# Groups of two experts instead of four: picks of 112 columns in two PSUM banks

## The chip, the cores and the metric

One Trainium2 chip, one of its cores. The metric is the device time of one execution in microseconds (us), from three runs of the kernel before. All arithmetic is float32.

## The reference, cut to what matters

A trunk of two residual layers (512 tokens, width 1024) and a final norm. Every layer has a mixer and then a mixture of experts (MoE). The change touches the MoE alone:

```
g_idx  = top1(softmax(xt @ router_group))            # one of 4 groups
e_idx  = top2(e_logits inside that group)            # two of its 8 experts
for each expert e of 32:                             # xb: the tokens that chose e
    hb = silu(xb @ w_gate[e]) * (xb @ w_up[e])       # 1024 -> 512, twice
    y  = hb @ w_down[e]                              # 512 -> 1024
out[token] = sum over its two experts of gate * y
```

w_gate, w_up and w_down are 2 MB each per expert, so each of the two layers streams 32 x 6.3 MB of weights.

## The kernel before, in words

Semaphores are written out by hand; every engine has its own program, and PSUM banks are handed over by two counters per bank (`fills` and `wait_full`, `drains` and `wait_drained`; `opens` waits for the last drain before a bank is used again).

**Weights.** Nine slots in SBUF (`ring`) hold three experts' gate, up and down matrices (`EXPERT_SLOTS`). SP issues all loads in order (`moe_loads`, L467): gate and up of expert e wait until PE has finished gate and up of expert e-3, down of e until down of e-3 is finished (L514 to L519). The loads of experts 3, 4 and 5 go out in pieces, released by half-way signals (`gu_half`) and by the same ends (L495 to L513).

**Picks.** An expert's tokens are gathered on PE: for each of 8 chunks of the width and each of 4 token tiles, h (the weights, 128x128 in two halves of 64) times a selection matrix (the moving side, CAP = 56 columns for each expert), summed over the tiles. DVE makes the selection matrices (`selections`, L1845; `select`, L1663: one instruction for each tile and expert) and copies the gathered chunks from PSUM, scaled, to `xgT` (`take_pick`, L1835). Experts are treated in groups of PICK = 4, so a pick has 224 columns; a bank holds 2 chunks, so 8 chunks take banks 0 to 3. `xgT` has two buffers, by the group's parity. While PE works through group g, it picks group g+1, one bank (2 chunks) per expert: five of the eight matmul steps before the expert's `turn`, three behind it, then `out_rows` (down). The selections of group g+2 are made at the end of group g on DVE (L1934).

**The start** differs. Group 0 is picked in two parts of 112 columns: part 0 (experts 0 and 1) while the router's tiles are worked out (`pick_first`, L697), part 1 (experts 2 and 3, banks named `second`) between the turns and downs of experts 0 and 1 and behind them (`first_experts`, L886). `slot_table` (L847) makes on PE the table of which row each result goes to, and DVE turns it into addresses (`row_table`, L1865). Group 1 is picked whole in experts 2 and 3.

**The expert loop** on PE (`expert`, L897): gate_up (L822; 8 chunks x 2 matrices of 512 columns), pick, turn (4 transposes), pick, down (L837; 4 chunks x 2). DVE (`dve_expert`, L1910): product with the silu that ACT made, copy of the turned hidden rows, take_pick, its half of the output rows, selections. POOL scatters the rows (L1499).

**The end.** The last four experts (`last_experts`, L963) overlap one expert's gate_up with the other's turn; nothing is picked there, since group 7 (experts 28 to 31) was picked during experts 24 to 27.

On PE a float32 matmul shows as two instructions, and a "pair" of half-width matmuls (two column halves of the array side by side) as four; one step of a pick is such a pair.

Of the kernel before, what the change touches and what calls it, by code (L numbers as in the profile page):

```python
# [50 lines left out]
PICK = 4  # L51
# [35 lines left out]
def trunk(nc, x, cols, final_g, ab_w_in, rg_w_a, rg_w_x, bias_rev, ab_w_out, c_w_in, c_w_out, router,  # L87
          w_gate, w_up, w_down, out):
    with ExitStack() as ctx:
# [79 lines left out]
        def half_row(row, nb):  # L169
# [24 lines left out]
        me.update(carve(high, [("sel", (NT, PICK * ROW)), ("rows", (2, D)), ("hT", (FC * CAP,)), ("silu", (F,)),  # L194
                               ("hrow", (F,)), ("tab", (3, NE)), ("B", (2, NT, NE))]))
        me.update(carve(low[:, 2 * NC * PICK * CAP:], [("A", (2, NT, CAP))]))
        me.update(carve(high[:, NT * PICK * ROW + D:], [("spread", (NT, NE))]))
# [5 lines left out]
        junk2 = me["sel"].rearrange("p a b -> p (a b)")  # L203
        late_sel = me["rows"][:, 0, 0:T].rearrange("p (t s) -> p t s", t=NT)
        late_pick = low[:, 0:T]
        hT_odd = low[:, T:T + FC * CAP]
        diag = low[:, T + FC * CAP:T + FC * CAP + 3 * P].rearrange("p (k t) -> p k t", k=3)
# [80 lines left out]
        def plan_moe(l):  # L288
# [303 lines left out]
        def _(pe):  # L592
# [104 lines left out]
            def pick_first(l, t, cs=range(NC), part=0):  # L697

                pe.wait_ge(sel_ready, (l * (NE // PICK + 3)) + t + 1)
                n = 2 * CAP  # L700
                for c in cs:
                    job = ("second", l, c // 2) if part else ("pick", l, 0, c // 2)
                    if t == 0 and c % 2 == 0:
                        opens(job)
                    mm = halves(bank(job)[:, (c % 2) * n:(c % 2 + 1) * n], h_cols(t, c),
                                hx["sel"][:, t, part * n:(part + 1) * n], t == 0 and c % 2 == 0, t == NT - 1 and c % 2 == 1)
                    if t == NT - 1 and c % 2 == 1:
                        fills(mm, job)

            def pick(l, g, b, steps):  # L710

                job = ("pick", l, g, b)
# [144 lines left out]
            def first_gate_up(l):  # L857

                for e in range(2):
# [3 lines left out]
                    for b in range(4):  # L863
                        if e == 0:
                            wait_drained(pe, ("pick", l, 0, b))
# [20 lines left out]
            def first_experts(l):  # L886

                first_gate_up(l)
                for e in range(2):
                    turn(l, e)  # L890
                    pick_first(l, e, part=1)
                    out_rows(l, e)
                pick_first(l, 2, part=1)
                pick_first(l, 3, part=1)
                slot_table(l)

            def expert(l, e):  # L897

                g, q = e // PICK, e % PICK
                three = EXPERT_SLOTS[e % 3]  # L900
                for s, k in e_in[l * NE + e][0:2]:
                    pe.wait_ge(ring_in[s], 16 * k)
                opens(("gu", l, e))
                if e == 2:
                    for b in range(4):
                        wait_drained(pe, ("second", l, b))
                    gate_up(l, three, g % 2, q, range(0, 4)).then_inc(gu_half, 1)
                    fills(gate_up(l, three, g % 2, q, range(4, 8)), ("gu", l, e))
                else:
                    if q == 0:  # L910
                        for b in range(4):
                            wait_drained(pe, ("pick", l, g, b))
                    fills(gate_up(l, three, g % 2, q), ("gu", l, e))
                if e == 3:
                    pick(l, 1, 2, range(0, 8))
                    turn(l, e)
                    pick(l, 1, 3, range(0, 8))
                    out_rows(l, e)
                    return
                b = 0 if e == 2 else q  # L920
                pick(l, g + 1, b, range(0, 5))
                turn(l, e)
                pick(l, g + 1, b, range(5, 8))
                out_rows(l, e)
                if e == 2:
                    pick(l, 1, 1, range(0, 8))
# [36 lines left out]
            def last_experts(l):  # L963

                a, b, c, d = range(NS, NE)
                for n in range(4):
# [9 lines left out]
                more_blocks(l)  # L976
                last_gate_up(l, c, range(0, 4))
# [74 lines left out]
            def moe(l):  # L1052
                pick_first(l, 3)
                first_experts(l)
                for e in range(2, NS):
                    expert(l, e)
# [531 lines left out]
        def _(dve):  # L1588
# [237 lines left out]
            def take_first(l, b, part):  # L1826

                job = ("second", l, b) if part else ("pick", l, 0, b)
# [435 lines left out]
```

## Time and profile before

| | |
|---|---|
| median of 3 runs | 1595.73 us (1593.35 to 1598.78) |
| the profiled execution | 1596.03 us, its span 1593.6 us |
| granted TensorE clock, mean | 0.994 |
| PE busy | 1537.7 us, 96% |
| DVE, ACT, POOL busy | 35%, 22%, 13% |
| DMA | 471.97 MB, mean 296 GB/s |

The span is what the profile covers; the 2.4 us between it and the execution's own time lie around it. The chain that ended last reaches back only through the final norm's last 3 us, so it does not tell what sets the time; the stages have to be read one by one. Layer 0's experts run from about 272 to 728 us, layer 1's from about 1115 to 1571 us. The two stretches are built alike.

### The profile page before, as it was taken

The page shows a single profiled execution, that of the slowest core. Times are in us where ns is not written, and L with a number is a line of the kernel's source. Part 1 is how long each engine was busy: PE and PEld are TensorE (multiplying, and loading weights), DVE is VectorE, ACT ScalarE, POOL GpSimd, SP SyncE. Part 2 cuts the span into 40 slices and gives each one's busy share as a digit, 9 for nine tenths or more (in the row PEclk, how much of TensorE's full clock was granted, in tenths as well). Part 3 has the DMA queues.
Part 4 walks back from the last instruction along what each step waited for, and adds up shares of the span by engine and source line. Part 5 has one row for each costly group of instructions (what it writes and reads, how often), then busy time and mean ns, then how long its engine had stood idle before and what let it go on. Part 6 is the DMA issues. An engine that isn't in the chain of part 4 may idle for free. (4 is left out here: it accounts for less than half of the span.)

```text
span 1593.6 us, 23381 instructions
## 1 busy us (share of the span) xinstructions
PE 1537.7 (96%) x9800; PEld 745.2 (47%) x9800; DVE 552.7 (35%) x1285; ACT 346.0 (22%) x577; POOL 210.4 (13%) x256
## 2 busy tenths in 40 slices
PE   7999999999999999988999999999999999999987
PEld 4444545544444444423566666645544444444422
DVE  4222636332222122125244444446332222122115
ACT  3131621100000000003444555432010000000003
POOL 5000000000000000000244444420000000000000
PEclk9999999999999999999999999999999999999999
DMA  8611056999999999997421112124999999999996
GB/s 314 247 62 53 27 229 273 409 367 426 428 427 427 427 426 427 427 422 316 185 81 54 54 62 95 58 95 183 375 360 427 427 426 427 427 427 428 426 422 275
DMA packets 59388, 471.97 MB, mean 296 GB/s; under 512 B 12929, under 2 KB 12937, under 8 KB 31376
## 3 DMA queue, kind: packets, MB, share of 16 engines
q1 hardware_dynamic: 54336, 462.51, 70.5%
q0 software_dynamic: 4800, 7.87, 1.3%
q8 instruction: 80, 1.31, 0.3%
q14 instruction: 28, 0.23, 0.0%
q10 hardware_dynamic: 144, 0.05, 0.0%
HBM read 452.03 MB, written 24.27 MB: 299 GB/s over the span
## 5 line engine op out<-in xcount | busy, mean ns | idle before, releaser
L827 PE MATMUL ps<-sb_ring,sb_work 128*56 128x512 f32 x2048 | 456.4, 598 | 21.1 <-issue 18.0
L827 PEld LDWEIGHTS ps<-sb_ring,sb_work 128*56 128x56 f32 x2048 | 147.6, 131 | 315.2 <-issue 314.8
L842 PE MATMUL ps<-sb_ring,sb_work 128*56 128x512 f32 x1024 | 230.9, 593 | 0.6 <-DMA sb_ring<-in_w_down_dram 0.6
L662 PE MATMUL ps<-sb_work,sb_h 128*64 128x224 f32 (+1 forms) x2304 | 218.1, 334 | 0.0
L1499 POOL DMA_INDIRECT expert_rows<-sb_work,sb_ri x60 | 54.9, 915 | 1118.2 <-DVE sb_work L1900 1105.5
L1891 DVE TENSOR_TENSOR sb_work<-sb_work,ps 56x512 f32<-56x512 f32 x64 | 69.3, 1083 | 336.3 <-ACT sb_work L1314 336.2
L662 PEld LDWEIGHTS ps<-sb_work,sb_h 128*64 128x64 f32 x2304 | 152.4, 137 | 63.9 <-issue 31.8
L1081 PE MATMUL ps<-sb_work,sb_ring 128*128 128x512 f32 x384 | 172.3, 603 | 2.0 <-ACT sb_work L1211 2.0
L1314 ACT ACTIVATE sb_work<-ps 56x512 f32<-56x512 f32 x64 | 37.7, 589 | 457.7 <-PE ps L827 457.7
L842 PEld LDWEIGHTS ps<-sb_ring,sb_work 128*56 128x56 f32 x1024 | 69.7, 130 | 119.4 <-issue 112.8
L1329 ACT ACTIVATE sb_work<-ps 56x512 f32<-56x512 f32 x60 | 35.5, 591 | 373.6 <-PE ps L842 373.6
L1081 PEld LDWEIGHTS ps<-sb_work,sb_ring 128*128 128x128 f32 x384 | 71.7, 191 | 86.9 <-issue 86.0
L735 PE MATMUL ps<-sb_work,sb_ring 128*128 128x512 f32 x256 | 110.3, 592 | 1.6 <-DVE sb_work L1611 1.6
L1900 DVE COPY sb_work<-ps 56x512 f32<-56x512 f32 x60 | 41.6, 693 | 191.2 <-ACT sb_work L1329 191.2
L735 PEld LDWEIGHTS ps<-sb_work,sb_ring 128*128 128x128 f32 x256 | 48.6, 190 | 62.6 <-issue 62.6
L2163 DVE COPY_PREDICATED sb_ring<-sb_tables,ps 128x512 f32<-128x512 uint32 x48 | 35.5, 740 | 93.0 <-PE ps L1099 92.2
L662 PE MATMUL ps<-sb_ring,sb_work 128*64 128x128 f32 x1120 | 64.3, 273 | 0.0
L662 PEld LDWEIGHTS ps<-sb_ring,sb_work 128*64 128x64 f32 x1120 | 60.9, 137 | 1.9 <-issue 1.9
L1548 POOL TENSOR_TENSOR sb_ring<-sb_ring 128x256 f32<-128x256 f32 x56 | 48.3, 863 | 88.9 <-ACT sb_ring L1384 50.4
L627 PE MATMUL ps<-sb_ring,sb_work 128*128 128x512 f32 x128 | 59.5, 599 | 0.0
L1665 DVE TENSOR_SCALAR sb_work<-sb_iota,sb_slot_key,sb_rstd 128x56 f32<-128x56 f32 x256 | 58.2, 302 | 0.3
L627 PE MATMUL ps<-sb_ring 128*128 128x512 f32 x128 | 57.8, 598 | 0.0
(241 smaller groups left out, 1198.6 us busy)
## 6 DMA issues: line engine op xcount, KB each, us to landing
sb_ring<-in_w_down_dram SPq DMA_DIRECT2D x62, 2048.0 KB, 23.5
sb_ring<-in_w_gate_dram SPq DMA_DIRECT2D x54, 2048.0 KB, 21.0
sb_ring<-in_w_up_dram SPq DMA_DIRECT2D x54, 2048.0 KB, 25.7
sb_ring<-in_w_gate_dram SPq DMA_DIRECT2D x18, 1024.0 KB, 10.7
sb_ring<-in_w_up_dram SPq DMA_DIRECT2D x18, 1024.0 KB, 28.8
sb_ring<-in_c_w_in_dram SPq DMA_DIRECT2D x8, 2048.0 KB, 8.8
sb_ring<-in_ab_w_in_dram SPq DMA_DIRECT2D x5, 2048.0 KB, 11.4
expert_rows<-sb_work SPq DMA_DIRECT2D x2, 4096.0 KB, 20.6
```

What stands on the lines that cost most here:

```text
L627: mm = nc.tensor.matmul(bank(job)[:], y[:, c, t * P:(t + 1) * P], wblock(s, NC)[:, c, :], start=(c == 0), stop=(c == NC - 1))
L662: mm = nc.tensor.matmul(dst[64 * z:64 * z + 64], a[:, 64 * z:64 * z + 64], b, start=start, stop=stop)
L735: mm = nc.tensor.matmul(dst[:], a, b, start=(c == 0), stop=(c == NC - 1))
L827: mm = nc.tensor.matmul(dst[64 * z:64 * z + CAP, :], me["xgT"][:, j, c, q * CAP:(q + 1) * CAP], wblock(slots[z], NC)[:, c, :], start=(c == ...
L842: mm = nc.tensor.matmul(dst[64 * z:64 * z + CAP, :], src[:, c * CAP:(c + 1) * CAP], wblock(slots[2], FC)[:, c, z * 512:(z + 1) * 512], sta ...
L1081: mm = nc.tensor.matmul(dst[:], w[:, c, k, :], xT[:, c, :], start=(c == 0), stop=(c == NC - 1))
L1314: A(me["silu"][64:64 + CAP, :], bank(("gu", l, e))[0:CAP, :], ACT.Silu).then_inc(silu_ready, 1)
L1499: return g.indirect_dma_start(out=y_d[l], out_offset=bass.IndirectOffsetOnAxis(ap=idx, axis=0), in_=me["rows"][0:CAP, j, :], in_offset=Non ...
L1548: g.tensor_tensor(qk[:, :, 0:m], kk[:, :, 0:m], e[:, :, 0:m], ALU.mult)
L1665: return v.tensor_scalar(dst, iota[:, 0:CAP], slot_key[:, t, e:e + 1], rstd[:, 2 * l + 1, t:t + 1], ALU.is_equal, ALU.mult)
L1891: return v.tensor_tensor(me["hrow"][0:CAP, :].rearrange("p (c q) -> p c q", c=FC), chunked(me["silu"][64:64 + CAP, :], FC), chunked(ps[moe ...
L1900: drains(v.tensor_copy(half_row(me["rows"][0:CAP, e % 2, :], 1), chunked(bank(("dn", l, e))[64:64 + CAP, :])), ("dn", l, e))
```

## The change

PICK becomes 2: a group is two experts, a pick has 112 columns, and a bank holds 4 chunks (CB), so 8 chunks take two banks (PB). One of these banks, 16 steps, is picked per expert. The cut of group 0 into two parts goes away: group 0 is now what part 0 was, and group 1 (experts 2 and 3) is an ordinary group picked in experts 0 and 1, all 16 steps between turn and down. From expert 2 on, 10 steps stand ahead of the turn and 6 behind it. `slot_table` moves behind expert 2's gate_up. The group of experts 30 and 31 is picked in `last_experts`, one bank behind the gate_up of each of experts 28 and 29, and DVE takes it there. The `sel` buffer is half as large, and a few buffers of the low region lie elsewhere.

```diff
-PICK = 4
+PICK = 2
+PB = 2
+CB = NC // PB
@@ plan_moe
             for g in range(NE // PICK):
-                for b in range(4):
+                for b in range(PB):
                     bk.add(("pick", l, g, b), moe_bank(l, b))
-                if g == 0:
-                    for b in range(4):
-                        bk.add(("second", l, b), moe_bank(l, b))
@@ pick
-                    c, t = 2 * b + i // NT, i % NT
-                    mm = halves(bank(job)[:, (c % 2) * PICK * CAP:(c % 2 + 1) * PICK * CAP], h_cols(t, c),
-                                me["sel"][:, t, 0:PICK * CAP], i == 0, i == 2 * NT - 1)
-                if steps[-1] == 2 * NT - 1:
+                    c, t = i // NT, i % NT
+                    mm = halves(bank(job)[:, c * n:(c + 1) * n], h_cols(t, CB * b + c), me["sel"][:, t, 0:n],
+                                i == 0, i == CB * NT - 1)
+                if steps[-1] == CB * NT - 1:
                     fills(mm, job)
@@ expert (PE), now for every e below NS; first_experts is gone
+            def expert(l, e):
+
+                g, q = e // PICK, e % PICK
+                if e >= 2:
+                    three = EXPERT_SLOTS[e % 3]
+                    for s, k in e_in[l * NE + e][0:2]:
+                        pe.wait_ge(ring_in[s], 16 * k)
+                    opens(("gu", l, e))
+                    if q == 0:
+                        for b in range(PB):
+                            wait_drained(pe, ("pick", l, g, b))
+                    mm = gate_up(l, three, g % 2, q, range(0, 4))
+                    if e == 2:
+                        mm.then_inc(gu_half, 1)
+                    fills(gate_up(l, three, g % 2, q, range(4, 8)), ("gu", l, e))
+                    if e == 2:
+                        slot_table(l)
+                    pick(l, g + 1, q, range(0, 10))
                     turn(l, e)
+                    pick(l, g + 1, q, range(10, 16))
                 else:
                     turn(l, e)
+                    pick(l, g + 1, q, range(0, 16))
                 out_rows(l, e)
@@ last_experts (PE)
                 last_gate_up(l, a, range(0, 8))
+                pick(l, NK // PICK, 0, range(0, 16))
                 last_gate_up(l, b, range(0, 4))
                 last_turn(l, a)
                 last_gate_up(l, b, range(4, 8))
+                pick(l, NK // PICK, 1, range(0, 16))
                 last_down(l, a, range(0, 3))
...
                 more_blocks(l)
+                for n in range(PB):
+                    wait_drained(pe, ("pick", l, NK // PICK, n))
                 last_gate_up(l, c, range(0, 4))
@@ take_pick (DVE)
-                g8 = fg[:, l, 2 * b:2 * b + 2].unsqueeze(2).broadcast_to([P, 2, PICK * CAP])
+                g8 = fg[:, l, CB * b:CB * b + CB].unsqueeze(2).broadcast_to([P, CB, PICK * CAP])
@@ dve_expert (DVE)
                 if e == 0:
                     hidden(l, 1)
+                take_pick(l, g + 1, q)
                 if e == 1:
                     slot_lists(l)
-                    for b in range(4):
-                        take_first(l, b, 1)
                     row_table(l)
-                if 2 <= e < NE - PICK:
-                    for b in {2: (0,), 3: (1, 2, 3)}.get(e, (q,)):
-                        take_pick(l, g + 1, b)
@@ moe (DVE)
-                for b in range(4):
-                    take_first(l, b, 0)
+                for b in range(PB):
+                    take_pick(l, 0, b)
```

## Rows read from the trace of the kernel before

**Rows 1.** The page's slices, 40 equal parts of the span: what the DMA engines moved.
```profile
GB/s 314 247 62 53 27 229 273 409 367 426 428 427 427 427 426 427 427 422 316 185 81 54 54 62 95 58 95 183 375 360 427 427 426 427 427 427 428 426 422 275
```

**Rows 2.** Timeline of PE, one expert of layer 0: start, us, line, count [idle before].
```profile
363.28 7.04 PE L827 MATMUL ps<-sb_ring,sb_work 128*56 128x512 f32 x32
370.15 2.06 PE L662 MATMUL ps<-sb_work,sb_h 128*64 128x224 f32 x20
372.22 0.42 PE L833 MATMUL ps<-sb_ident,sb_work 56*128 56x56 f32 x4
372.57 1.35 PE L662 MATMUL ps<-sb_work,sb_h 128*64 128x224 f32 x12
373.76 3.60 PE L842 MATMUL ps<-sb_ring,sb_work 128*56 128x512 f32 x16
377.19 7.04 PE L827 MATMUL ps<-sb_ring,sb_work 128*56 128x512 f32 x32
```

**Rows 3.** The same timeline: gate_up of experts 25 and 28.
```profile
628.46 7.08 PE L827 MATMUL ps<-sb_ring,sb_work 128*56 128x512 f32 x32 [0.75 <-issue]
...
673.64 7.08 PE L827 MATMUL ps<-sb_ring,sb_work 128*56 128x512 f32 x32 [1.21 <-DMA sb_ring<-in_w_up_dram]
```

**Rows 4.** Windows: stretch, us, engines' busy us (instructions), PEclk, DMA share, GB/s.
```profile
320.00:325.00 5.00, 5.00 (x26) 1.50 (x22) 0.00 (x0) 0.00 (x0) 0.00 (x0) 1.00 0.74 291
325.00:330.00 5.00, 5.00 (x52) 3.44 (x50) 1.99 (x3) 0.59 (x1) 0.00 (x0) 1.00 0.69 229
```

**Rows 5.** Timeline of SP's DMA issues, layer 0, experts 5 (down), 6 and 7.
```profile
315.76 0.33 SPq L458 DMA_DIRECT2D sb_ring<-in_w_down_dram  x1
325.65 0.33 SPq L458 DMA_DIRECT2D sb_ring<-in_w_gate_dram  x1
...
335.68 0.33 SPq L458 DMA_DIRECT2D sb_ring<-in_w_down_dram  x1
342.54 0.33 SPq L458 DMA_DIRECT2D sb_ring<-in_w_gate_dram  x1
```

**Rows 6.** Timeline of PE at the start of layer 0's experts.
```profile
264.12 1.13 PE L662 MATMUL ps<-sb_rt,sb_work 128*64 128x36 f32 x32
265.05 1.76 PE L662 MATMUL ps<-sb_work,sb_h 128*64 128x112 f32 x32
...
269.38 3.29 PE L662 MATMUL ps<-sb_work,sb_h 128*64 128x112 f32 x64
272.50 13.90 PE L827 MATMUL ps<-sb_ring,sb_work 128*56 128x512 f32 x64
...
300.44 0.41 PE L851 MATMUL ps<-sb_work,sb_ones 128*128 128x32 f32 x2
...
301.52 0.64 PE L827 MATMUL ps<-sb_ring,sb_work 128*56 128x512 f32 x1
```

**Rows 7.** Timeline of DVE, layer 0: first take, slot table, output rows, selections of one group.
```profile
271.64 1.47 DVE L1832 TENSOR_TENSOR sb_work<-ps,sb_fg 128x224 f32<-128x224 f32 x4 [0.16 <-PE ps L662]
...
301.82 0.19 DVE L1870 TENSOR_REDUCE sb_top<-ps 128x1 f32<-128x32 f32 x1 [0.89 <-PE ps L853]
...
303.04 0.69 DVE L1900 COPY sb_work<-ps 56x512 f32<-56x512 f32 x1
...
312.33 0.62 DVE L1842 TENSOR_TENSOR sb_work<-ps,sb_fg 128x448 f32<-128x448 f32 x1 [0.90 <-PE ps L662]
...
336.98 3.61 DVE L1665 TENSOR_SCALAR sb_work<-sb_iota,sb_slot_key,sb_rstd 128x56 f32<-128x56 f32 x16
```

**Rows 8.** Timeline of PE in the last experts, layer 0 (683 to 703), layer 1 (1547).
```profile
683.88 5.34 PE L827 MATMUL ps<-sb_ring,sb_work 128*56 128x512 f32 x16 [3.16 <-issue]
...
689.53 3.65 PE L827 MATMUL ps<-sb_ring,sb_work 128*56 128x512 f32 x16
...
702.91 10.66 PE L827 MATMUL ps<-sb_ring,sb_work 128*56 128x512 f32 x48 [2.34 <-issue]
...
1547.25 12.21 PE L827 MATMUL ps<-sb_ring,sb_work 128*56 128x512 f32 x48 [3.17 <-issue]
```

More of the change, by code:

```diff
@@ L193, in trunk @@
         me = carve(low, [("xgT", (2, NC, PICK * CAP))])
-        me.update(carve(high, [("sel", (NT, PICK * ROW)), ("rows", (2, D)), ("hT", (FC * CAP,)), ("silu", (F,)),
+        me.update(carve(high, [("junk", (D,)), ("rows", (2, D)), ("hT", (FC * CAP,)), ("silu", (F,)),
                                ("hrow", (F,)), ("tab", (3, NE)), ("B", (2, NT, NE))]))
+        me.update(carve(high, [("sel", (NT, PICK * ROW))]))
         me.update(carve(low[:, 2 * NC * PICK * CAP:], [("A", (2, NT, CAP))]))
-        me.update(carve(high[:, NT * PICK * ROW + D:], [("spread", (NT, NE))]))
+        me.update(carve(high[:, 2 * D:], [("spread", (NT, NE))]))
         fin_g = tables[:, 0:D]
@@ L695, in positions, with pick_first @@
                 fills(mm, ("pos", l, t))
-            def pick_first(l, t, cs=range(NC), part=0):
+            def pick_first(l, t, cs=range(NC)):
                 pe.wait_ge(sel_ready, (l * (NE // PICK + 3)) + t + 1)
-                n = 2 * CAP
+                n = PICK * CAP
                 for c in cs:
-                    job = ("second", l, c // 2) if part else ("pick", l, 0, c // 2)
-                    if t == 0 and c % 2 == 0:
+                    job = ("pick", l, 0, c // CB)
+                    if t == 0 and c % CB == 0:
                         opens(job)
-                    mm = halves(bank(job)[:, (c % 2) * n:(c % 2 + 1) * n], h_cols(t, c),
-                                hx["sel"][:, t, part * n:(part + 1) * n], t == 0 and c % 2 == 0, t == NT - 1 and c % 2 == 1)
-                    if t == NT - 1 and c % 2 == 1:
+                    mm = halves(bank(job)[:, (c % CB) * n:(c % CB + 1) * n], h_cols(t, c), hx["sel"][:, t, :],
+                                t == 0 and c % CB == 0, t == NT - 1 and c % CB == CB - 1)
+                    if t == NT - 1 and c % CB == CB - 1:
                         fills(mm, job)
             def pick(l, g, b, steps):
-                job = ("pick", l, g, b)
+                job, n = ("pick", l, g, b), PICK * CAP
                 if steps[0] == 0:
@@ L863, in first_gate_up @@
                     for b in range(4):
-                        if e == 0:
-                            wait_drained(pe, ("pick", l, 0, b))
+                        if e == 0 and b % 2 == 0:
+                            wait_drained(pe, ("pick", l, 0, b // 2))
                         mm = gate_up(l, EXPERT_SLOTS[e], 0, e, (2 * b, 2 * b + 1), 6 if e else 7)
@@ L884, in out_rows @@
                 fills(down(l, EXPERT_SLOTS[e % 3]), ("dn", l, e))
[L886 to L895, printed above, removed]
             def expert(l, e):
                 g, q = e // PICK, e % PICK
[L900 to L904, printed above, removed]
-                    for b in range(4):
-                        wait_drained(pe, ("second", l, b))
-                    gate_up(l, three, g % 2, q, range(0, 4)).then_inc(gu_half, 1)
-                    fills(gate_up(l, three, g % 2, q, range(4, 8)), ("gu", l, e))
-                else:
-                    if q == 0:
-                        for b in range(4):
[L912 to L915, printed above, removed]
-                    turn(l, e)
[L917 to L923, printed above, removed]
@@ L924, in expert @@
                 out_rows(l, e)
-                if e == 2:
-                    pick(l, 1, 1, range(0, 8))
             def last_gate_up(l, e, cs):
@@ L976, in last_experts @@
                 more_blocks(l)
+                for n in range(PB):
+                    wait_drained(pe, ("pick", l, NK // PICK, n))
                 last_gate_up(l, c, range(0, 4))
@@ L1053, in moe @@
                 pick_first(l, 3)
-                first_experts(l)
-                for e in range(2, NS):
+                first_gate_up(l)
+                for e in range(NS):
                     expert(l, e)
@@ L1823, in _ @@
             mixer_end(0)
-            def take_first(l, b, part):
-                job = ("second", l, b) if part else ("pick", l, 0, b)
-                wait_full(dve, job)
-                n = 2 * CAP
-                g8 = fg[:, l, 2 * b:2 * b + 2].unsqueeze(2).broadcast_to([P, 2, n])
-                drains(v.tensor_tensor(me["xgT"][:, 0, 2 * b:2 * b + 2, part * n:(part + 1) * n],
-                                       bank(job)[:, 0:2 * n].rearrange("p (c s) -> p c s", c=2), g8, ALU.mult), job)
             def take_pick(l, g, b):
@@ L1958, in last_experts @@
                 last_turned(l, a)
+                take_pick(l, NK // PICK, 0)
                 last_hidden(l, b)
                 last_turned(l, b)
+                take_pick(l, NK // PICK, 1)
                 out_rows(l, a)
```

17 lines of the change are left out of this document (8 added, 9 removed).

## The prediction

> **What bounds the kernel now.** The page says PE 96% busy, which invites the wrong answer. I read the 40 slices next: in both stretches of experts the DMA engines moved 422 to 428 GB/s in slice after slice, nine in the first [rows 1]. So PE and the weight stream are both near their limit, and only the timeline tells which one ends last. Early on, PE goes from one expert's gate_up to the next in 377.19 - 363.28 = 13.91 us with no idle time [rows 2]. Later, from expert 25 to 28, it takes (673.64 - 628.46) / 3 = 15.06 us, and PE is idle 0.75 to 1.21 us ahead of the gate_up, which ends with the load of the up matrix [rows 3]. An expert's weights are three loads of 2048 KB, 6.29 MB, and 6.29 MB at 427 GB/s [rows 1] are 14.7 us. So PE asks for weights faster than they come from the start, lives on what the ring holds, and has used it up some 20 experts later. From then on the **weight stream sets the end** of each MoE, and PE's idle time in it (ten us or so per layer) costs nothing. What counts is how early the stream becomes unbroken. It is not unbroken at first: between 320 and 330 us it moved 291 and 229 GB/s [rows 4].
>
> **The picks themselves.** Before, an expert's share of picks is 32 instructions of 224 columns: 372.22 - 370.15 plus 373.76 - 372.57 = 3.26 us, 102 ns each [rows 2]. After, it is 64 of 112 columns. The trace has those: 64 took 272.50 - 269.38 = 3.12 us, 49 ns each [rows 6]. So 3.1 to 3.2 against 3.26: nothing lost, 0.1 us of PE won per expert, hidden behind the stream. Columns in all are the same. Twice as many weight loads is no bound, since 32 instructions of the same form with 36 columns went by in 265.05 - 264.12 = 0.93 us, 29 ns each, loads included [rows 6].
>
> The Trainium skill (TensorE: Matmul & The Clock Gate, Back-to-back issue gap) says that in a stream of weight load and matmul pairs 128 columns sustain about 81 ns per matmul, because the load counts too. By that an estimate for 64 of them is 5.2 us. The row disagrees, at 49 ns for 112; it is a rival below.
>
> DVE takes 448 columns per expert before and after (0.62 us), on the same place behind the turn [rows 7]; selections are half as many, twice as often. Both lie under gate_up (6.87 us, 363.28 to 370.15) and down (3.43 us) [rows 2]. Cost nothing; if that cover were gone, 0.62 per two experts. POOL's scatters and SP's order of loads are unchanged.
>
> **Start of a MoE.** (a) Gate_up of expert 0 waited for a first take of 224 columns that needed two chunks; now it needs four chunks and a take of 0.62 us. Four chunks are full 0.8 us into the last tile's pick, which is 1.56 us long; with the 0.3 us that the first take lagged in the trace and 0.62 it is 0.2 us late: bounds 0 and 0.4, I take **+0.2**. Halved selections in the router's stage save DVE time ahead of a wait for PE: nothing.
> (b) Expert 0 and 1: the picks between turn and down are 64 instructions each instead of 32, and the 64 behind down of expert 1 go. Same sum. slot_table (301.52 - 300.44 = 1.1 us) leaves too [rows 6], so gate_up of expert 2 starts at about 300.4 instead of 301.5 and ends at 307.3.
> (c) Then slot_table, to 308.4, and then **a new wait**. The pick of group 2 needs its selections. On DVE these stand behind row_table, which waits for slot_table, and behind expert 1's output rows. From slot_table's start to DVE's first instruction it is 301.82 - 300.44 = 1.38 us, row_table 303.04 - 301.82 = 1.22, output rows 0.66, eight selections half of 3.61 = 1.8: 5.1 us, of which PE works 1.1. PE waits **4.0 us**, till 312.4. Queued behind it on PE: turn, pick and down of expert 2; SP then issues expert 5's down late. DVE needs expert 2's hidden product (1.1 us) next, ready before the turn.
> (d) After idle times of 3.16 and 3.17 us PE ran slow for a while: 5.34 against 3.65 us for 16 instructions, 12.21 against 10.66 for 48; after 2.34 us it did not [rows 8]. So the wait costs a further 0 to 1.6 us; as 4.0 is longer than 3.16, likelier the latter.
> (e) Removed from experts 2 and 3: half their picks, 6.5 us (they picked four experts' worth, now two). Net by the start of expert 4: PE is 1.1 + 6.5 - 1.1 - 4.0 - (0 to 1.6) = 2.5 to 0.9 us ahead, less (a).
>
> **What this does to the stream.** Loads go out when PE ends something [rows 5]. After (without (a)): down of 2 ends 312.4 + 3.6 (pick, turn, pick) + 3.4 = 319.4, with the slow clock 321.0; SP 0.2 later. Then +6.87 for gate_up of 3, +7.0 for its rest, +6.87 for gate_up of 4. The issues:
>
> expert 5 down: 315.76 before, 319.6 to 321.2 after.
> expert 6 gate, up: 325.65, then 326.5 to 328.1.
> expert 6 down: 335.68, then 333.5 to 335.1.
> expert 7 gate, up: 342.54, then 340.4 to 342.0.
>
> Now the queue. 291 GB/s over 5 us are 3.4 us of flow, so it ran dry at 323.4; 229 GB/s are 2.7 us, so flow resumed at 327.3, 1.7 us after the issue [rows 4, 5]. A 2 MB load flows 4.9 us. Before: 6 gate and up 327.3 to 337.1, down to 342.0, then idle to 342.54 + 1.7 = 344.2, unbroken from there. After: without expert 5's down the queue is dry at 318.5; that load flows from 321.3 (322.9) to 326.2 (327.8); 6 gate and up from 328.2 (329.8) to 338.0 (339.6); down follows at once to 342.9 (344.5), and 7 gate and up follows at once. So the unbroken stream starts 1.3 us earlier, or 0.3 later. With (a): -1.1 to +0.5. I take **-0.4 us per layer**, near the middle because (d) leans late while the small dips of a short queue, which I don't count, lean early. Layer 1 is built alike.
>
> **End of a MoE.** The pick of experts 30 and 31 moves here, 2 x 3.15 us of PE. The first falls in the idle 3.16 us ahead of expert 29's gate_up, the second is made up in the idle 2.34 (3.17) us ahead of expert 30's [rows 8]. In layer 0 that is 6.3 us of work against 5.5 of idle time; but with the first gap filled the slow clock behind it (1.7 us) goes too, so gate_up of 30 waits for its weights as before: 0. If that cover were gone, 6.3 us per layer. The loads for expert 31's down, released by down of 28 some 1.4 us later, still find a full queue.
>
> **Sum:** 2 x (-0.4) = -0.8 us on the profiled 1596.03, so 1595.2; the median of the runs is 0.3 lower, 1595.73, which gives 1594.9. I say **1595.0**. Bounds of the costs: -2.2 to +1.0. The runs spread by 2 to 3 us on either side, and about 0.3% (4.8 us) is what a measurement can tell from no change.
>
> **Rivals.**
> 1. *Faster* (0.12): the wait in (c) is cheaper, or moved work keeps the queue from running dry at all. The idle flow to be won is 3.9 us plus 2.2 us per layer by the sum above; all of it is 12 us: 1584. Half is 1590. For: PE is ahead by expert 4. Against: expert 5's down is issued late by exactly the wait.
> 2. *Slower* (0.10): the moved picks aren't covered at the end. Place: PE in the last four experts. Price: up to 6.3 us per layer, 12.6 in all, 1608; if only the second pick is exposed, 3.15 each, 1602. It decides when PE reaches expert 29 with less than about 1 us of idle ahead, that is if the ring isn't used up by then. Against: PE waits for weights from expert 25 at the latest [rows 3].
> 3. *Slower, weight loads bound the picks* (0.02). The point is a period of 15 us: 6.87 + 0.36 + 3.43 = 10.66 without picks, so 64 instructions must take 4.3 us, 68 ns each. If one of 112 columns took what one of 224 takes, 102 ns, the period would be 17.2, and the 23 experts from 5 to 27 cost 23 x (17.2 - 13.9) = 76 us, less the ten that PE idles now: 66 per layer, 1728. By the 81 ns of the Trainium skill (the same page and section) it is an estimate of 15.8 us per expert, some 35 per layer, about 1666. The trace speaks against both, with 49 ns.
> 4. *The change doesn't do what it says*: were the wait in (c) absent because DVE had its selections ready, -2.9 per layer from (c) to (e) would be capped by the queue, 1591; it is part of 1.
>
> **Numbers.** My forecast 0.76. The likeliest cases give 1592.5 to 1597.5 with the runs' spread; reaching to half of rival 1 and of rival 2's smaller price, 1590.5 to 1599.5. Chances: faster 0.13, same 0.75, slower 0.12.
>
> **What the profile would show.** Right: 64 instructions of 112 columns in 3.1 to 3.2 us per expert and a period of about 13.85 us, later 15.0 to 15.1; PE idle about 4 us per layer behind slot_table, ended by DVE's selections; the flow broken near 319 us and again near 327, whole from about 328; no gap ahead of expert 29's gate_up. Wrong: a longer period at the end, gate_up of 30 later in relation to 29's, or an unbroken stream from 300 us on.

## The result and the profile after

| | before | after |
|---|---|---|
| median | 1595.69 us (1593.35 to 1598.78, 7 runs) | 1600.95 us (1598.27 to 1603.03, 7 runs) |
| ratio to before | 1 | 1.003, 95% interval 1.0018 to 1.0042 |
| the profiled execution, its span | 1596.03, 1593.6 us | 1600.95, 1598.6 us |
| granted TensorE clock, mean | 0.994 | 0.994 |

The forecast was 1595.0 with 1590.5 to 1599.5; the change costs 5.3 us, 0.3%, and lies 1.4 us above the range. The times of the parts that I looked at most were right. PE's timeline behind expert 1 of layer 0, which answers to [rows 2, 6], and two rows of layer 1:

```profile
300.45 7.04 PE L828 MATMUL ps<-sb_ring,sb_work 128*56 128x512 f32 x32
307.42 0.41 PE L852 MATMUL ps<-sb_work,sb_ones 128*128 128x32 f32 x2
...
312.56 4.00 PE L663 MATMUL ps<-sb_work,sb_h 128*64 128x112 f32 x40 [3.79 <-DVE sb_work L1653]
316.49 0.67 PE L834 MATMUL ps<-sb_ident,sb_work 56*128 56x56 f32 x4
317.09 1.97 PE L663 MATMUL ps<-sb_work,sb_h 128*64 128x112 f32 x24
...
322.33 7.03 PE L828 MATMUL ps<-sb_ring,sb_work 128*56 128x512 f32 x32
329.20 2.08 PE L663 MATMUL ps<-sb_work,sb_h 128*64 128x112 f32 x40
...
331.61 1.37 PE L663 MATMUL ps<-sb_work,sb_h 128*64 128x112 f32 x24
...
336.24 1.03 PE L828 MATMUL ps<-sb_ring,sb_work 128*56 128x512 f32 x4
...
1158.38 3.62 PE L663 MATMUL ps<-sb_work,sb_h 128*64 128x112 f32 x40 [3.75 <-DVE sb_work L1653]
...
1552.65 12.21 PE L828 MATMUL ps<-sb_ring,sb_work 128*56 128x512 f32 x48 [2.90 <-issue]
```

Gate_up of expert 2 starts at 300.45 (300.4 was forecast), the wait for DVE's selections is 3.79 us (4.0), it ends at 312.56 (312.4). Behind it the same 68 instructions that take 2.08 + 0.42 + 1.37 us an expert later take 4.00 + 0.67 + 1.97: the slow clock costs 2.8 us (the granted clock of 315 to 320 us is 0.66, below: part of this stretch ran at 1.2 instead of 2.4 GHz). Gate_up of expert 3 follows at 322.33; before it was 318.57.

What SP issued and what the DMA engines then moved (columns as in [rows 4]); they answer to [rows 4, 5]:

```profile
322.54 0.33 SPq L459 DMA_DIRECT2D sb_ring<-in_w_down_dram  x1
329.41 0.33 SPq L459 DMA_DIRECT2D sb_ring<-in_w_gate_dram  x1
...
336.45 0.33 SPq L459 DMA_DIRECT2D sb_ring<-in_w_down_dram  x1
343.32 0.33 SPq L459 DMA_DIRECT2D sb_ring<-in_w_gate_dram  x1
```

```profile
315.00:320.00 5.00, 5.00 (x52) 3.92 (x50) 1.02 (x2) 0.00 (x0) 0.00 (x0) 0.66 0.73 294
320.00:325.00 5.00, 5.00 (x26) 1.56 (x24) 0.69 (x1) 2.40 (x4) 0.00 (x0) 1.00 0.31 69
325.00:330.00 5.00, 5.00 (x40) 2.05 (x38) 0.00 (x0) 1.56 (x2) 0.91 (x1) 1.00 0.89 375
330.00:335.00 5.00, 5.00 (x68) 3.32 (x66) 2.84 (x8) 0.01 (x1) 0.00 (x0) 1.00 0.96 342
```

There are two gaps, as the prediction had it, but each issue is 1.3 us later than the late end of its range (321.2, 328.1, 335.1, 342.0), and so the second gap reaches beyond 330 us, where the prediction had the flow whole from about 328.

Two moments of each MoE tell where the time went: the start of gate_up of expert 28, which waits for its up matrix, and the first instruction of the late add (L1005 before, L993 after), both counted from the start of gate_up of expert 0. Ahead of them stands what the DMA engines moved in the 60 us from the 30th to the 90th behind that start. As windows (the last number is GB/s; times 60 us it is MB), first before, then after, layer 0 and 1:

```profile
302.50:362.50 60.00, 59.98 (x396) 28.72 (x394) 17.92 (x48) 6.91 (x10) 4.75 (x5) 1.00 0.95 382
1144.60:1204.60 60.00, 59.99 (x396) 28.77 (x394) 17.92 (x49) 6.92 (x10) 4.62 (x5) 1.00 0.94 376
```

```profile
302.61:362.61 60.00, 56.21 (x468) 29.19 (x466) 17.46 (x50) 6.91 (x10) 4.76 (x5) 0.94 0.91 370
1148.47:1208.47 60.00, 56.23 (x474) 28.60 (x472) 17.47 (x50) 6.92 (x10) 4.63 (x5) 0.97 0.93 380
```

The same for the kernels of this study that bear on it (layer 0 / layer 1; "in all" is the median against the before of the same session):

| kernel | MB moved, 30 to 90 us | gate_up of 28 | late add | in all, us |
|---|---|---|---|---|
| before | 22.92 / 22.56 | 401.14 / 403.23 | 456.24 / 458.31 | |
| after | 22.20 / 22.80 | 404.35 / 403.20 | 460.09 / 459.83 | +5.3 |
| after again | 22.62 / 22.56 | 403.34 / 404.00 | 459.17 / 460.90 | +5.0 |
| table first | 24.78 / 24.96 | 399.08 / 398.29 | 453.67 / 456.31 | -5.5 |
| selections early | 24.36 / 24.48 | 398.73 / 399.12 | 454.58 / 454.91 | -1.6 |
| before, with a wait | 20.28 / 20.52 | 407.20 / 407.39 | 462.43 / 462.53 | +11.4 |
| before, picks split | 22.38 / 22.80 | 403.11 / 402.77 | 459.04 / 457.14 | +1.6 |
| after, no end picks | 22.02 / 22.62 | 404.30 / 403.31 | 459.69 / 457.91 | +1.2 |
| table first, no end picks | 24.60 / 24.72 | 398.79 / 399.47 | 453.43 / 454.56 | -4.9 |
| before, no overflow branch | 22.74 / 22.98 | 401.15 / 402.96 | 456.80 / 460.27 | -1.5 |
| after, no overflow branch | 22.44 / 22.68 | 403.20 / 403.49 | 458.34 / 457.93 | +3.4 |
| before, more waits on TensorE | 22.98 / 23.16 | 402.74 / 402.19 | 458.49 / 455.97 | +0.1 |

For the change the late add comes on average 2.7 us later (459.96 against 457.28), and again 2.8 in the repeat: two layers make 5.4 to 5.5 us, which is the difference of the medians. So nothing that costs time lies outside the two MoEs. These are readings of one execution each: before's own two layers, built alike, differ by 2.1 us at gate_up of 28 and at the late add. So a difference of less than about 1 us in one row of the table proves little; the means of the repeat agree with the first profile's to 0.1 us.

### The profile page after: what moved, and what is told of

It reads as the page before. It is cut to its first block, busy times and chain, and to the rows that moved or that the text cites. A ratio compares the mean times of both kernels' runs of the same rounds, so it can differ in the third digit from the quotient of the medians.

```text
span 1598.6 us, 26973 instructions
## 1 busy us (share of the span) xinstructions
PE 1541.1 (96%) x11592; PEld 794.2 (50%) x11592; DVE 554.0 (35%) x1277; ACT 346.0 (22%) x577; POOL 211.0 (13%) x256
## 3 DMA queue, kind: packets, MB, share of 16 engines
q8 instruction: 94, 1.54, 0.4%
## 4 chain that ended last, share of the span: by engine, by line
PE 49%; DMA 3%; DVE 2%; issue 1%; ACT 1%; POOLq 0%; SPq 0%; DVEq 0%; ACTq 0%
PE ps L828 13%; PE ps L663 11%; PE ps L1069 11%; PE ps L843 6%; PE ps L628 4%; DMA sb_ring<-in_w_up_dram 2%; PE ps L1087 2%; DMA sb_ring<-expert_rows 1%; PE ps L834 1%; PE ps L1128 0%; PE ps L993 0%; DVE sb_h L2027 0%; PE ps L1004 0%; ACT sb_work L1199 0%; PE ps L1096 0%
## 5 line engine op out<-in xcount | busy, mean ns | idle before, releaser
L663 PE MATMUL ps<-sb_work,sb_h 128*64 128x112 f32 x4096 | 224.3, 263 | 7.5 <-DVE sb_work L1653 7.5
L663 PEld LDWEIGHTS ps<-sb_work,sb_h 128*64 128x64 f32 x4096 | 206.5, 139 | 42.2 <-issue 30.8
L1821 DVE TENSOR_TENSOR sb_work<-ps,sb_fg 128x448 f32<-128x448 f32 x64 | 40.0, 625 | 58.4 <-PE ps L663 58.1
## 6 DMA issues: line engine op xcount, KB each, us to landing
sb_ring<-in_w_gate_dram SPq DMA_DIRECT2D x18, 1024.0 KB, 10.8
```

Source lines behind the costliest of these rows:

```text
L663: mm = nc.tensor.matmul(dst[64 * z:64 * z + 64], a[:, 64 * z:64 * z + 64], b, start=start, stop=stop)
L1821: drains(v.tensor_tensor(me["xgT"][:, g % 2, CB * b:CB * b + CB, :], bank(job)[:, 0:CB * PICK * CAP].rearrange("p (c s) -> p c s", c=CB), ...
```

## The experiments

**Where the wait stands.** slot_table goes back ahead of expert 2's gate_up, as it stood before; all else is the changed kernel.

```diff
                 g, q = e // PICK, e % PICK
+                if e == 2:
+                    slot_table(l)
                 if e >= 2:
                     three = EXPERT_SLOTS[e % 3]
...
                     fills(gate_up(l, three, g % 2, q, range(4, 8)), ("gu", l, e))
-                    if e == 2:
-                        slot_table(l)
                     pick(l, g + 1, q, range(0, 10))
```

> The changed kernel with slot_table put back ahead of gate_up of expert 2, so that DVE's row_table, output rows and selections run under that gate_up. T1 (the new wait of PE behind slot_table, 3.8 us per layer and 1.5 to 2.8 us of slow clock behind it, sends the loads of experts 5 to 7 late and so sets the whole loss): the wait is gone, down of expert 2 ends near 315 us instead of 322, gate_up of 3 near 322.5; the weight stream is unbroken some 3 us per layer earlier than in the kernel before. Time about 1590, against 1595.7 before and 1601 for the changed kernel. T2 (the picks moved into the last four experts set the loss): the wait goes, but the time stays at 1599 to 1601. T3 (picks in 112 columns slow the stream or PE by themselves): 1598 to 1601.

1590.14 us (1588.61 to 1591.33), ratio 0.9965 (0.9952 to 0.9978). PE's timeline:

```profile
300.45 0.41 PE L852 MATMUL ps<-sb_work,sb_ones 128*128 128x32 f32 x2
...
308.45 2.16 PE L663 MATMUL ps<-sb_work,sb_h 128*64 128x112 f32 x40
...
315.60 7.04 PE L828 MATMUL ps<-sb_ring,sb_work 128*56 128x512 f32 x32
```

No wait, no slow clock, gate_up of expert 3 at 315.60 instead of 322.33, and 24.9 MB in the opening 60 us instead of 22.5. 2.4 MB at 427 GB/s are 5.6 us per layer; the late add comes 5.0 earlier, twice that is 10, the medians differ by 10.8. So moving that one table decides the sign of the change: with it in its old place the groups of two are 0.35% faster than before, and this is the fastest kernel of the study, together with its variant without end picks.

**The wait shortened.** In the changed kernel the selections of group 2 are made on DVE ahead of `slot_lists`, in the time in which DVE was idle.

```diff
@@ dve_expert
                 if e == 1:
+                    selections(l, 2)
                     slot_lists(l)
...
-                if q == PICK - 1 and g + 2 < NE // PICK:
+                if q == PICK - 1 and e > 1 and g + 2 < NE // PICK:
```

> The changed kernel with the eight selections of group 2 made ahead of slot_lists instead of behind row_table and the output rows; slot_table stays behind gate_up of expert 2. T1: the pick follows slot_table at once; the next wait is at the turn of expert 2, for DVE's hidden product, which stands behind row_table, the output rows: about 1 us, too short for the slow clock. Time 1591 to 1592, nearly as with the table put first (1590.1). Against T1: 1597 or more.

1593.58 us (1590.17 to 1597.2, 12 runs), ratio 0.999 (0.998 to 0.9999). What is left is a wait at the turn, for the hidden product, which stands behind the table on DVE:

```profile
312.00 0.43 PE L834 MATMUL ps<-sb_ident,sb_work 56*128 56x56 f32 x4 [1.22 <-DVE sb_work L1870]
```

The turn's four instructions at 0.43 us are at the full clock: 1.22 us of idle time don't bring the slow one. Its row in the table promises more than 1.6 us; but the profiled execution took 1590.25 us and was among the fastest of the twelve, so the row flatters it. By the ratios the leftover wait costs 0.25% against the kernel with the table first (0.999 and 0.9965), 4.0 us.

**The wait alone.** The kernel before, with a wait of about the same length at the same place: 40 more selections on DVE, for which PE waits behind expert 2's gate_up.

```diff
@@ expert (PE), behind gate_up
+                if e == 2:
+                    pe.wait_ge(again, l + 1)
@@ dve_expert, e == 1
+                    for n in range(40):
+                        q2 = n // NT % PICK
+                        ins = select(l, n % NT, PICK + q2, me["sel"][:, n % NT, q2 * CAP:(q2 + 1) * CAP])
...
+                    ins.then_inc(again, 1)
```

> The kernel before with a wait put in behind gate_up of expert 2: DVE repeats 40 selections (same values) after expert 1's output rows, and PE waits for them ahead of the pick, about 4 us and the slow clock behind it. T1: a late start of the loads passes into the end one for one, as nothing else is removed: 6 us per layer, 1605 to 1608. If the ring's reserve absorbed such a wait (against T1): 1596 to 1598.

1607.01 us (1604.05 to 1611.85), ratio 1.0077 (1.006 to 1.0094): 11.4 us for two waits.

```profile
313.97 3.68 PE L663 MATMUL ps<-sb_work,sb_h 128*64 128x224 f32 x20 [4.16 <-DVE sb_work L1668]
```

3.68 instead of 2.06 us [rows 2]: 1.6 us of slow clock. 4.16 + 1.6 = 5.8 per layer, 11.6 in all; 11.4 are measured, with 9.6 to 15 by the interval. The opening moved 2.3 MB less, 5.5 us, and the late add is 5.2 us later. **Time that PE loses here passes almost whole into the end**, although PE idles for ten us per layer later on.

**The picks' width alone.** The kernel before, each pick of 224 columns as two of 112.

```diff
@@ pick
-                    mm = halves(bank(job)[:, (c % 2) * PICK * CAP:(c % 2 + 1) * PICK * CAP], h_cols(t, c),
-                                me["sel"][:, t, 0:PICK * CAP], i == 0, i == 2 * NT - 1)
+                    n, at0 = 2 * CAP, (c % 2) * PICK * CAP
+                    for k in range(2):
+                        mm = halves(bank(job)[:, at0 + k * n:at0 + (k + 1) * n], h_cols(t, c),
+                                    me["sel"][:, t, k * n:(k + 1) * n], i == 0 and k == 0, i == 2 * NT - 1 and k == 1)
```

> The kernel before with every pick of 224 columns issued as two of 112, everything else as it was (experts 4 to 31; as many instructions and weight loads as in the changed kernel, the same place and banks). T1 and T2: no difference that can be measured, 1595 to 1596.5; PE's distance between experts stays at 13.9 us. T3: this alone makes 1598 to 1601.

1597.24 us (1594.48 to 1599.46), ratio 1.0009 (1.0 to 1.0017). PE's timeline of one expert; the next gate_up is 13.94 us behind the first:

```profile
363.13 7.04 PE L829 MATMUL ps<-sb_ring,sb_work 128*56 128x512 f32 x32
370.00 2.09 PE L662 MATMUL ps<-sb_work,sb_h 128*64 128x112 f32 x40
372.08 0.42 PE L835 MATMUL ps<-sb_ident,sb_work 56*128 56x56 f32 x4
372.44 1.37 PE L662 MATMUL ps<-sb_work,sb_h 128*64 128x112 f32 x24
```

On PE the halves cost nothing, as the prediction said. Yet all together they may: up to 0.17%. The table shows a trace of it. Take the MB of the opening at 427 GB/s as the time by which gate_up of 28 should move against before (means of the two layers). The two kernels with 224 columns come out at -0.4 (before with a wait) and +0.2 us (before without the branch). The eight profiles with 112 columns come out later than that by 0.4 to 1.5 us, 0.9 on average.

**Is it the code?** The picks are twice as many instructions, and these have to be fetched: the page's instruction queue q8 shows 94 packets and 1.54 MB after, 80 and 1.31 before, and 95 with the picks split. Three kernels add satisfied waits to the kernel before, on one engine each.

```diff
@@ GpSimd, behind each scatter
+                    for _ in range(192):
+                        pool.wait_ge(made, 1)
```

> The kernel before with 192 further instructions on GpSimd behind the scatter of each expert, each a wait that is satisfied already. They move no data and compute nothing; their code has to be fetched. What it is for: the kernel with halved picks and nothing else (3592 instructions more on TensorE's side) was 1.0009 times before, with an interval of 1.0 to 1.0017. Theory A: the fetch of code takes its share of the weight stream. Then three times as many added instructions cost three times as much, 3 to 6 us (1599 to 1602), the profile's instruction queue shows about 0.7 MB more than its 1.31 MB, and gate_up of expert 28 in layer 1 starts 1.5 us or more later in relation to expert 0 than before's 403.2. Theory B: the fetch costs nothing that can be seen and the 1.5 us of the halved picks are something else: 1595 to 1597, ratio 1.000, the relative start of gate_up(28) unchanged.

1616.46 us (1613.57 to 1618.71), ratio 1.0126 (1.011 to 1.0141): 20.7 us, far more than theory A had. The loads that SP issued between 500 and 560 us, before and here (where they are issued, and issue to landing):

```profile
L458 SPq DMA_DIRECT2D sb_ring<-in_w_down_dram x5: 327/328/328, 502.6 to 558.2; - x5
...
DMA to landing us min/median/max: 23.4/27.1/31.5
```

```profile
L458 SPq DMA_DIRECT2D sb_ring<-in_w_down_dram x5: 328/328/328, 502.7 to 558.4; - x5
...
DMA to landing us min/median/max: 27.5/32.5/38.1
```

Issued at the same times, with 427 and 428 GB/s moved in that stretch, they land 5.4 us later; by expert 28 gate_up is 9.4 us behind in layer 0 and 6.7 in layer 1. So the bytes flow, but not those that the next load needs to be complete.

```diff
@@ ScalarE, act_expert
+                if e >= 2:
+                    for _ in range(192):
+                        act.wait_ge(slots_hot, l + 1)
```

> The kernel before with 192 satisfied waits per expert on ScalarE, which is busy 4 us in 50 there; the same number on GpSimd cost 20.7 us for 45 more packets of code of 8 KB, 0.37 MB, which at the rate of the stream (427 GB/s) would be 0.9 us. Theory A1: a packet of code goes through one of the 16 DMA engines, and every weight load ends when the last of the engines has ended its share, so a byte of code costs as much as 16 bytes spread over all. By that 0.37 MB cost 14 us on one engine, 20.7 with what waits behind each; the same on ScalarE costs 10 to 22 us, if its code comes through an engine that is as loaded as the others. Theory A2: the cost hangs on the one engine behind GpSimd's queue, which has the scatter to carry too; ScalarE's code costs 0 to 3 us. Theory C: the waits hold up GpSimd itself and its scatters, and it is not the code: 0 here, and the number of code packets rises all the same.

1612.67 us (1611.68 to 1614.37), ratio 1.0105 (1.009 to 1.012). The number is what theory A1 gave, but the number alone is a trap, for PE waits for something else:

```profile
506.96 2.06 PE L662 MATMUL ps<-sb_work,sb_h 128*64 128x224 f32 x20
509.83 0.42 PE L833 MATMUL ps<-sb_ident,sb_work 56*128 56x56 f32 x4 [0.82 <-DVE sb_work L1894]
...
690.61 10.47 PE L827 MATMUL ps<-sb_ring,sb_work 128*56 128x512 f32 x48
```

ScalarE's silu comes late behind its own added waits, DVE's product after it, and PE's period is 14.6 to 14.7 us. Gate_up of 28 (with the first half of 29's) follows at 690.61 without a wait, so PE's start does not tell what the loads did; their landings in the trace do. Counted from the start of gate_up of expert 0 as in the table, the up matrix of expert 28 has landed (layer 0 / layer 1) at:

| kernel | up of 28 landed, us | code packets more than before |
|---|---|---|
| before | 400.90 / 402.99 | |
| waits on GpSimd | 410.28 / 409.65 | 45 on q14, 0.37 MB |
| waits on ScalarE | 411.19 / 409.66 | 39 on q14, 0.32 MB |
| waits on TensorE (next run) | 402.50 / 401.95 | 6 on q8, 0.10 MB |

With the waits on ScalarE the loads lag as they do with the waits on GpSimd, again at an unchanged rate (426 GB/s from 500 to 560 us, 427 from 600 to 660). So it is not GpSimd's place in front of its scatters (C), and A2's 0 to 3 us doesn't hold for the loads; the page counts the code of both engines on the same queue, q14. A1 is left standing for q14. As a price for every byte of code it does not: by its 14 us for 0.37 MB, an estimate, the 15 packets of 16 KB more on q8 would cost the split picks 9 us, and these measured 1.6. And of the 16.6 us here the loads' lag and PE's own period can't be told apart, since PE is 3.4 and 4.9 us later than the load that it would otherwise wait for.

```diff
@@ expert (PE), at its end
+                if e >= 5:
+                    for _ in range(64):
+                        pe.wait_ge(sel_ready, 1)
```

> The kernel before with 64 satisfied waits per expert on TensorE, experts 5 to 27 of both layers, behind the work of each expert, where TensorE has 1.1 us of idle time per expert to lose before it falls behind the weights. It asks what TensorE's own code costs, which is what the halved picks add. Theory A (the fetch of TensorE's code slows the stream): the more packets on its queue cost what the 15 packets of the halved picks did (1.6 us, interval 0 to 2.7) in proportion to their number. Theory B: TensorE's code costs nothing, and the time stays at 1595 to 1597. Where the waits themselves take more than 1.1 us per expert the period shows it, and the kernel is slower by that; then only the start of the loads tells.

1596.13 us (1594.49 to 1598.31, 12 runs), ratio 1.0004 (0.9996 to 1.0013), with 6 code packets more on q8. No cost that the measurement can tell; the interval doesn't exclude 0.6 us (6/15 of 1.6) either. By the measure used for the split picks (opening against gate_up of 28) its loads are 1.0 us late too, with 224 columns. That speaks for the code and against the columns as the cause, but it is one profile, and a cost that is the same for 6 packets as for 15 fits no simple price. What makes loads of the 112-column kernels late by 0.9 us per layer **stays open**.

**The picks at the end.** The changed kernel with the two picks of `last_experts` cut from 16 steps to one each; the rows of experts 30 and 31 are not computed.

```diff
-                pick(l, NK // PICK, 0, range(0, 16))
+                pick_one(l, NK // PICK, 0)
...
-                pick(l, NK // PICK, 1, range(0, 16))
+                pick_one(l, NK // PICK, 1)
```

> The changed kernel with the two picks in the last four experts cut to one of their 16 steps each (the gathered rows of experts 30 and 31 are left out, the rest stands). T1: they were covered by waits for weights, so 1600 to 1601. T2: 1596 or below, with gate_up of expert 30 about 1.5 us earlier after the start of its MoE. T3: nearly as T1, at most 0.5 us less.

1596.8 us (1596.14 to 1599.37, 11 runs), ratio 1.0013 (1.0004 to 1.0022). Between the ratios of the changed kernel (1.003, and 1.0027 in the repeat below) and this one lie 2.2 to 2.7 us, though their intervals still meet; the late adds differ by 0.4 us in layer 0 and 1.9 in layer 1, together 2.3. With the table first as well:

> Table put first and, besides, the two picks of the last four experts cut to one of their 16 steps (rows of experts 30 and 31 left out). If the two costs add, as one is at the start and one at the end of a MoE: 1590.1 less 2 to 4 us, 1586 to 1588. If the end picks only cost while the stream is late: 1590.

1590.25 us (1588.95 to 1591.25), ratio 0.9964 (0.9951 to 0.9977), against 0.9965 with the picks. There they cost nothing that shows. So the two costs do not simply add, and the profile of this kernel does not say where the 2 us between the late adds of layer 1 (454.56 and 456.31) are made up in the medians.

**Why layer 1's end is not covered.** Ahead of expert 30's gate_up PE idles 3.17 us in layer 1 [rows 8] and still 2.90 after, though 6.3 us of picks were put in front of it. An idle time that new work does not shorten is hardly a wait for weights, and the trace of before has the landings: the halves of gate and up that this gate_up starts with were in at 1542.23, PE was through with down at 1544.08, and it started at 1547.25. At this place stands the branch for experts with more than 56 tokens (`more_blocks`: a wait for a flag, the load of the flag, and the jump over the block), not taken with these inputs. Both kernels without that branch, and without the loads that belong to it:

```diff
-            more_loads(0)
-            more_loads(1)
...
-                more_blocks(l)
```

> The kernel before without the branch over the overflow blocks (more_blocks on all engines, more_loads on SP; it is not taken with these inputs). T4: in layer 1 the 2.9 to 3.3 us of idle PE ahead of gate_up of expert 30 are the jump over that block and not a wait for weights, since they stood the same length behind expert 29's down in every run so far: the gap goes or shrinks to below 1.5 us, and the time falls by 1 to 3 us. T5 (they are a wait for the loads of expert 30): the gap stays at about 3 us and the time at 1595 to 1596.

> The changed kernel without that branch. T4: the moved second pick then fills a real wait for weights or none is left; 3 to 4 us less than the changed kernel (1597 to 1598), more than the kernel before wins by the same edit. T5: 1600 to 1601.

Before without it: 1593.69 us (1592.21 to 1597.22, 11 runs), 0.9987 (0.9978 to 0.9996). After without it: 1598.5 (1596.69 to 1601.4, 11 runs), 1.002 (1.0012 to 1.0029). PE in layer 1, the first and then the second:

```profile
1539.72 4.50 PE L840 MATMUL ps<-sb_ring,sb_work 128*56 128x512 f32 x20
1544.05 7.18 PE L825 MATMUL ps<-sb_ring,sb_work 128*56 128x512 f32 x32
1553.13 3.65 PE L825 MATMUL ps<-sb_ring,sb_work 128*56 128x512 f32 x16 [1.90 <-issue]
...
1564.50 2.51 PE L840 MATMUL ps<-sb_ring,sb_work 128*56 128x512 f32 x6 [2.13 <-DMA sb_ring<-in_w_down_dram]
```

```profile
1544.07 4.50 PE L841 MATMUL ps<-sb_ring,sb_work 128*56 128x512 f32 x20
1548.41 7.04 PE L826 MATMUL ps<-sb_ring,sb_work 128*56 128x512 f32 x32
```

Gate_up of 30 now follows down directly in both: the idle 3 us belonged to the branch. In the first of these executions, the slowest of its eleven, all of the gain is lost again behind it, to waits for weights (its late add is later than before's in the table). By the ratios over all runs the branch cost 2.1 us in the kernel before (0.6 to 3.5 by the interval) and 1.1 to 1.6 us in the changed one. T4 was right on the idle time, but it expected the changed kernel to win more than the kernel before, and it won no more.

The branch has no fixed price. In layer 0 the changed kernel has no idle time there, and the kernel before has 2.34 us [rows 8]. In the kernel with more waits on TensorE it is the other way round, 3.36 us in layer 0 and none in layer 1:

```profile
706.68 5.77 PE L827 MATMUL ps<-sb_ring,sb_work 128*56 128x512 f32 x18 [3.36 <-issue]
...
1541.89 4.50 PE L842 MATMUL ps<-sb_ring,sb_work 128*56 128x512 f32 x20
1546.22 7.09 PE L827 MATMUL ps<-sb_ring,sb_work 128*56 128x512 f32 x32
```

In layer 1 of the kernels before and after, a packet of 16 KB on q8 moves inside the gap (1544.59 to 1545.66, and 1550.11 to 1551.20), and PE resumes 1.6 and 1.5 us behind it; in layer 0 of the changed kernel such a packet had moved 5 us before PE came there. That fits a wait for the code behind the jump, but such packets also move where PE does not stop, and no run tells the flag's load, the jump and the fetch apart.

**Once more.** The changed kernel, unaltered.

> The changed kernel once more, unaltered, beside before on the same chip: 1.003 times before (1.002 to 1.004) by its first measurement. All theories expect 1599.5 to 1602. The kernel without the end picks gave 1.0013 against before in another session, 4 us less than the changed kernel, of which its profile shows only about 2; if this repeat comes out at 1.002 or less, part of these 4 us is the difference between sessions.

1600.74 us (1598.24 to 1603.02, 10 runs), ratio 1.0027 (1.0017 to 1.0036).

```profile
313.37 3.41 PE L663 MATMUL ps<-sb_work,sb_h 128*64 128x112 f32 x40 [3.79 <-DVE sb_work L1653]
```

The wait is the same to 0.01 us; the slow clock behind it is not: 3.41 + 0.67 + 1.42 us here against 3.87 without it, 1.6 us, where the first profile had 2.8.

## Why the prediction was wrong

By its own steps, in us per layer, mean of the two layers, from the first profile and the repeat:

| step | predicted | measured |
|---|---|---|
| stream through the opening ((a) to (e)) | -0.4, bounds -1.1 to +0.5 | +0.6, +0.4 |
| loads later still, by gate_up of 28 | not in the sum | +1.0, +1.1 |
| end of the MoE | 0 | +1.1, +1.3 |
| sum | -0.4 | +2.7, +2.8 |

(First row: 22.50 and 22.59 MB against 22.74, at 427 GB/s. Second: gate_up of 28 at 403.78 and 403.67 against 402.19, less the first row. Third: the rest to the late add.) Between forecast and measurement lie 3.1 to 3.2 us per layer, and the three rows have about a third each.

**The picks, (a), (b), (c): right.** 64 instructions took 3.1 to 3.2 us as one block, the period is 13.93 us instead of 13.91 (13.85 was forecast); (a) came to 0.3 us (3.41 from the last pick's start to gate_up after, 3.12 before), the wait and its place to 0.2 us. The 81 ns of the Trainium skill (TensorE: Matmul & The Clock Gate, Back-to-back issue gap) are not what this chip shows for 112 columns, and rival 3 is out.

**(d), the slow clock: mis-sized.** It said 0 to 1.6 us from two rows of another place, and chose the middle of the stream's range. Four waits in the two profiles of the changed kernel cost 2.8, 1.6, 1.6 and 1.7 us, two in the kernel with a wait 1.6 and 1.7: the upper end is the normal case. With it alone the prediction's own sum gives an unbroken stream 0.5 us later, which is what was measured on average. The 2.8 of layer 0 fits with that layer's opening losing 1.7 us (0.72 MB) in the first profile, while layer 1's gained 0.6. Its criterion, the length of the idle time, does not hold either: ahead of gate_up of 29 in layer 0, 16 instructions took 5.14 us behind 2.40 us of idle time (table first, no end picks; granted clock 0.62) and 3.65 us behind 3.15 (before, with a wait; granted clock 1.00).

**(e), PE ahead by expert 4: too hopeful.** PE was 0.8 us late in layer 0 (336.24 against 335.47) instead of 0.9 to 2.5 ahead; in layer 1, and in both layers of the repeat, it was 0.4 to 0.5 us ahead, counted from the start of gate_up of expert 0. Expert 3, with half its picks gone, made up 3 us, as computed; it had more to make up.

**A missing term.** That the picks' split costs nothing on PE was right, and I took this for the whole price. Split picks alone cost 1.6 us (0 to 2.7) in all, through loads that land later; by what path is open.

**The end of a MoE: the step that failed.** "The second is made up in the idle 2.34 (3.17) us ahead of expert 30's" took idle time labelled "issue" for a wait for weights. In layer 1 it belongs to the branch: 2.90 us stand there after, 3.17 before, and the second pick of 3.1 us is partly exposed: gate_up of 30 comes 31.0 us behind that of 28 instead of 29.4, 1.6 us later (1.8 in the repeat). In layer 0 it was right but for 0.7 us. Taking both picks away gives 2.3 us back by the profiles. This is rival 2's effect, at the place that it names and at less than half of its smaller price; the condition that it set (a ring not yet used up) did not come in, so its "against" (PE waits for weights from expert 25 on) was true and not enough. The prediction's own mark, "gate_up of 30 later in relation to 29's", is what the trace shows.

**Rival 1** was not this kernel, but the idle flow that it names was there: with the table first, the change gives 5.5 us, about what "half is 1590" stood for.

## What to carry to other kernels

When an unbroken stream of transfers sets the end, a stage's later idle time covers nothing that delays the stream's start: a wait of 4.2 us put early into each layer cost its full length and the slow clock behind it, while work put under idle time near the end cost little. Before new work is hidden under an idle stretch, ask what ends that stretch: "issue" can be a branch that is not taken, as here, which the new work does not shorten. And when a step that feeds a slower engine's chain is moved, here a table of 1.1 us, count the chain behind it: moved back, it turned 0.3% slower into 0.35% faster.

## What the runs showed of the hardware that was not expected

- A branch that is not taken, over a large block, came with 2.9 to 3.4 us of idle PE in layer 1 of every kernel that had it but one; the kernel with more waits on TensorE had none there and 3.36 us in layer 0, where the changed kernel had none. Without the branch the idle time was gone. What decides in which layer it stands was not tested.
- 192 satisfied waits per expert on GpSimd, which otherwise issues one scatter per expert, made weight loads land 5.4 us later at an unchanged 427 GB/s and cost 20.7 us; on ScalarE they made the loads as late. The mean rate does not tell when a given load is complete.
- The slow clock behind the same wait of 3.8 us took 1.6 us in one execution and 2.8 in another; behind 1.2 us of idle time it did not come, behind 2.40 us it came in one kernel, and behind 3.15 us it did not in another.
